# Top rounds ahead of the rotation in attention, first squares ahead of a rounding, retention's last 16 keys as stacked rounded parts

## The reference, cut to what matters

```python
def gated_deltanet_group(q, k, v, ...):
    qkv = jax.nn.silu(causal_depthwise_conv(jnp.concatenate([q, k, v], -1), conv_w))
    ...
    q = l2norm(q.reshape(b, t, DN_HEADS, DN_HEAD_K)) * (DN_HEAD_K ** -0.5)
    k = l2norm(k.reshape(b, t, DN_HEADS, DN_HEAD_K))
...
def dsa_attention(...):                       # 8 heads, one choice of keys for all
    score = jnp.where(admissible[None], score, -jnp.inf)
    _, sel = lax.top_k(score, k_top)          # k_top = 128 of 512 keys for each query
    p = jax.nn.softmax(...)                   # over the 16 meta keys and the chosen ones
...
def retention(q, k, v):                       # 4 heads, 528 keys, values 512 wide
    # y[q] = sum over keys k <= q of decay**(q - k) * (q . k) * v[k]
    y = y * lax.rsqrt(jnp.mean(y * y, axis=-1, keepdims=True) + EPS)
...
y = rmsnorm_2(h, final_norm)
return y[:, N_META:]
```

## Time and profile before

| | |
|---|---|
| median of 3 runs | 2015.24 us (2015.1 to 2015.66) |
| the profiled execution | 2013.44 us, of which the span is 2011.6 us |
| granted TensorE clock, mean over the span | 0.998 |
| PE busy | 1988.7 us, 99% |
| POOL, DVE, ACT busy | 939.3, 861.9 and 738.4 us |

### The profile page before, as it was taken

The page is one execution under the profiler, slowest core; times in us unless marked ns, Lnnn a source line. Parts: engine busy times, 40 slices in busy tenths (PEclk is TensorE's granted clock), DMA queues, the critical chain, the costliest instruction groups (busy, mean ns, idle before and its releaser), DMA issues.

```text
span 2011.6 us, 30211 instructions
## 1 busy us (share of the span) xinstructions
PE 1988.7 (99%) x11374; PEld 1703.1 (85%) x11374; DVE 861.9 (43%) x1495; ACT 738.4 (37%) x1124; POOL 939.3 (47%) x1220
## 2 busy tenths in 40 slices
PE   9999999999999999999999999999999999999998
PEld 6788777899999998788998888888888888888887
DVE  7844776722222225976442243343334552222112
ACT  5633555522222224534444242323333332222222
POOL 6332211554545655453332545354544665454564
PEclk9999999999999999999999999999999999999999
DMA  5211111232222322231111312222222222222222
GB/s 200 74 63 51 37 36 37 74 105 85 92 94 86 103 97 102 74 104 44 65 66 55 125 53 96 78 90 74 89 84 74 94 94 90 98 93 95 95 104 84
DMA packets 49898, 168.68 MB, mean 84 GB/s; under 512 B 6416, under 2 KB 8592, under 8 KB 49808
## 3 DMA queue, kind: packets, MB, share of 16 engines
q1 hardware_dynamic: 46336, 161.37, 23.8%
q10 hardware_dynamic: 3472, 6.03, 0.9%
HBM read 165.29 MB, written 2.10 MB: 83 GB/s over the span
## 4 chain that ended last, share of the span: by engine, by line
PE 92%; DVE 5%; ACT 1%; issue 1%; DMA 0%; DVEq 0%; ACTq 0%
PE slot L2077 91%; DVE qkv L1444 1%; DVE x_lo L1855 0%; DVE xt L1847 0%; PE slot L2523 0%; DVE qkv L1441 0%; PE slot L2257 0%; PE slot L2222 0%; DVE slot L1438 0%; DMA small<-small_in 0%; ACT mixed_hi L947 0%; DVE square L1838 0%; DVE ix_score L1885 0%; DVE xt L1403 0%; DVE top L1881 0%
## 5 line engine op out<-in xcount | busy, mean ns | idle before, releaser
L2599 POOL TENSOR_TENSOR w_lo<-w_raw,w_hi 128x256 fp32r<-128x256 f32 x1216 | 939.1, 805 | 1061.7 <-ACT w_hi L826 803.0
L2077 PE MATMUL slot<-x_hi,w_hi 128*128 128x264 f32 (+1 forms) x1864 | 641.4, 344 | 0.9 <-DVE x_lo L1855 0.7
L2077 PE MATMUL slot<-x_hi,w_lo 128*128 128x264 f32 (+1 forms) x1864 | 629.3, 338 | 0.0
L2077 PE MATMUL slot<-x_lo,w_hi 128*128 128x264 f32 (+1 forms) x1864 | 627.7, 337 | 0.0
L2077 PEld LDWEIGHTS slot<-x_hi,w_hi 128*128 128x128 f32 x1864 | 350.9, 188 | 48.5 <-issue 8.0
L2077 PEld LDWEIGHTS slot<-x_hi,w_lo 128*128 128x128 f32 x1864 | 350.9, 188 | 38.1 <-issue 1.8
L2077 PEld LDWEIGHTS slot<-x_lo,w_hi 128*128 128x128 f32 x1864 | 350.0, 188 | 39.1
L826 ACT ACTIVATE w_hi<-w_raw 128x1024 fp32r<-128x1024 f32 x215 | 225.4, 1054 | 314.6 <-PE slot L2077 306.9
L2077 PE MATMUL slot<-f_hi,w_hi 128*128 128x264 f32 (+2 forms) x550 | 173.5, 316 | 0.0
L2077 PE MATMUL slot<-f_hi,w_lo 128*128 128x264 f32 (+2 forms) x550 | 173.3, 315 | 0.0
L2077 PE MATMUL slot<-f_lo,w_hi 128*128 128x264 f32 (+2 forms) x550 | 172.9, 314 | 0.0
(11 more groups left out here) (351 smaller groups left out, 2863.6 us busy)
## 6 DMA issues: line engine op xcount, KB each, us to landing
w_raw<-weights SPq DMA_DIRECT2D x303, 512.0 KB, 3.2
h<-x_t ACTq DMA_DIRECT2D x4, 512.0 KB, 6.2
dec<-decays ACTq DMA_DIRECT2D x4, 264.0 KB, 3.2
const<-consts SPq DMA_DIRECT2D x1, 576.0 KB, 6.3
at_rot<-rotations ACTq DMA_DIRECT2D x1, 528.0 KB, 5.3
ix_rot<-rotations ACTq DMA_DIRECT2D x1, 528.0 KB, 6.6
rt_rot<-rotations ACTq DMA_DIRECT2D x1, 528.0 KB, 3.8
w_raw<-weights SPq DMA_DIRECT2D x2, 256.0 KB, 4.1
```

The source lines that it names most:

```text
L2077: return nc.tensor.matmul(out, lhsT, rhs, start=start, stop=stop)
L2599: nc.gpsimd.tensor_tensor(w_lo[j][:, piece], w_raw[j][:, piece], w_hi[j][:, piece].bitcast(F32), ALU.subtract).then_inc(s_lo, 1)
```

## The change

1. Attention: of the 8 late rounds of `top([3])` two now stand ahead of step 0, one in each of the steps 0 to 4 ahead of the projections of that step, and one behind those of step 0. `admit(3)` moves from step 4 to step 5.
2. First projections: ACT makes the squares of tiles 0 and 1 ahead of the rounding `x_high(1, 5, M)`.
3. Retention: the matmul for the last 16 keys takes rounded parts. Two new tiles hold them one above the other at partitions 0, 32 and 64: values hi, hi, lo and scores hi, lo, hi, with zeros between. It has 96 rows and is of the short form. DVE gets two memsets once and, for each head, four small instructions; ACT gets two copies of 16x512 for each head; PE gets a wait for them at the first value tile.
4. The end: the halves stay. The table load for `Ln` and `Exp` moves ahead of the last projection, the rounding of the last (padding) weight block behind the last `Exp`, and with it POOL's four pieces. The second half is multiplied as 4, 2, 1 and 1 tiles of 256 columns, where it was 2, 2, 3 and 1, and stored as 4, 2 and 2, the first of the stores by SP.

```diff
-OUT_PARTS = [(0, 2), (2, 4), (4, KD - 1), (KD - 1, KD)]
+LAST_COLS = [(0, 256), (256, T)]
+OUT_PARTS = [[(0, 2), (2, 4), (4, KD - 1), (KD - 1, KD)], [(0, 4), (4, 6), (6, KD - 1), (KD - 1, KD)]]
+OUT_MADE = [sum(len(parts) for parts in OUT_PARTS[:a]) for a in range(len(OUT_PARTS))]
+STORES = [[(0, 2), (2, 4), (4, KD - 1), (KD - 1, KD)], [(0, 4), (4, 6), (6, KD)]]
...
-TOP_LATE = {0: 2, 1: 2, 2: 2, 3: 1, 4: 1}
+TOP_AHEAD = 2
+TOP_WITHIN = {0: 1, 1: 1, 2: 1, 3: 1, 4: 1}
+TOP_BEHIND = {0: 1}
+ADMIT_STEP = 5
...
                 else:
+                    nc.scalar.preload_act_table_set(LN_EXP)
                     for j in range(KD - 1):
...
-                    w_split(BLOCKS_PADDED - 1)
...
                 if j >= 3:
                     x_high(1, j - 3, M)
+            A.sync()
+            squares(srcs[0:2])
             ahead(("qkv", 8))
             x_high(1, 5, M)
-
-            A.sync()
-            squares(srcs[0:2])
...
+                        act.wait_ge(s_rst, 5 * hd + 5)
+                        act.wait_ge(s_last, hd + 1)
+                        A.sig(nc.scalar.activation(rvm_parts[32:32 + M, :], rvm[0:M, :], ACT.Copy), s_rvmhi, 2 * hd + 1)
+                        A.sig(nc.scalar.activation(rvm_parts[0:M, :], rvm[0:M, :], ACT.Copy), s_rvmhi, 2 * hd + 2)
                     made["table"] = None
                     copy_out(("rg", hd, j), rg[j], ACT.Silu)
...
+            w_split(BLOCKS_PADDED - 1)
+            a, (c0, c1) = len(LAST_COLS) - 1, LAST_COLS[-1]
+            for k0, k1 in STORES[a][1:]:
+                act.wait_ge(s_y, out_made(a, k1))
+                act.dma_start(out_dram[:, k0:k1, c0:c1], h[:, k0:k1, M + c0:M + c1]).then_inc(s_out, 16)
...
             admit(2)
+            for _ in range(TOP_AHEAD):
+                top([3])
             for s in range(ATT_STEPS + 3):
...
+                for _ in range(TOP_WITHIN.get(s, 0)):
+                    top([3])
                 for key, _ in filled(s):
                     projected(key)
-                for _ in range(TOP_LATE.get(s, 0)):
+                for _ in range(TOP_BEHIND.get(s, 0)):
                     top([3])
-                if s == max(TOP_LATE):
+                if s == ADMIT_STEP:
                     admit(3)
...
+                V.own(nc.vector.tensor_copy(rstm_parts[0:M, :], rstm[0:M, :]))
+                V.own(nc.vector.tensor_copy(rstm_parts[64:64 + M, :], rstm[0:M, :]))
+                V.sync()
+                V.own(nc.vector.tensor_tensor(rstm_parts[32:32 + M, :], rstm[0:M, :], rstm_parts[0:M, :].bitcast(F32), ALU.subtract))
+                dve.wait_ge(s_rvmhi, 2 * hd + 2)
+                V.sig(nc.vector.tensor_tensor(rvm_parts[64:64 + M, :], rvm[0:M, :], rvm_parts[0:M, :].bitcast(F32), ALU.subtract),
+                      s_last, hd + 2)
...
-                    m = mm(ps[:, T - M:T], rvm[0:M, d * P:d * P + P], rstm[0:M, 0:M], False, True)
+                    if d == 0:
+                        pe.wait_ge(s_last, hd + 2)
+                    m = mm(ps[:, T - M:T], rvm_parts[0:96, d * P:d * P + P], rstm_parts[0:96, 0:M], False, True)
```

More of the change, by code:

```diff
@@ L204, in ffn_results @@
         if (i, d) == (2, KD - 1):
-            add(("down", i, "first half"))
-            add(("norm", 4))
+            for a in range(len(LAST_COLS) - 1):
+                add(("down", i, ("part", a)))
+                add(("norm", 4 + a))
         add(("down", i, d), 3)
@@ L742, in build, with out_made @@
         rs0, squares0 = dsz[:, 0, :], [dqk[:, k, :] for k in range(KD)]
+        def out_made(a, k):
+            return OUT_MADE[a] + sum(k1 <= k for _, k1 in OUT_PARTS[a])
         def halves(ap):
@@ L1320, in _ @@
             ffn(2, M)
-            for a in range(2):
+            act.wait_ge(s_rsd, made["rs"])
+            for a, (c0, c1) in enumerate(LAST_COLS):
                 key = ("norm", 4 + a)
-                if a == 0:
-                    nc.scalar.preload_act_table_set(LN_EXP)
-                    act.wait_ge(s_rsd, made["rs"])
                 wait_result(act, key)
-                half = rs[0][:, a * 256:a * 256 + 256]
-                A.sig(nc.scalar.activation(half, slot(key)[:, 0:256], ACT.Ln, bias=eps[:, 0:1], scale=1.0 / D), *evac_at(key))
+                part = rs[0][:, c0:c1]
+                A.sig(nc.scalar.activation(part, slot(key)[:, 0:c1 - c0], ACT.Ln, bias=eps[:, 0:1], scale=1.0 / D), *evac_at(key))
                 A.sync()
[L1330 to L1333, removed]
-            act.wait_ge(s_out, 16 * 2 * len(OUT_PARTS))
+                A.sig(nc.scalar.activation(part, part, ACT.Exp, scale=-0.5), s_rs, made["rs"] + a + 1)
+            w_split(BLOCKS_PADDED - 1)
[3 more added lines that the diff above has]
+                act.dma_start(out_dram[:, k0:k1, c0:c1], h[:, k0:k1, M + c0:M + c1]).then_inc(s_out, 16)
+            act.wait_ge(s_out, 16 * sum(len(stores) for stores in STORES))
         @block.vector
@@ L2381, in ffn, with part_sum, beside @@
                     down(j, 0, ("down", i, j), parts)
-                middle = M + T // 2
-                def half_sum(a, last):
+                def part_sum(a, last):
+                    c0, c1 = LAST_COLS[a]
                     ps = begin(("norm", 4 + a)) if not last else slot(("norm", 4 + a))
                     pe.wait_ge(s_acc, SQUARES_BEFORE_LAST + 2 * (KD - 1) + (a + 1 if last else 0))
-                    m = mm(ps[:, 0:256], K("ones"), square[0 if last else 1][:, a * 256:a * 256 + 256], not last, last)
+                    m = mm(ps[:, 0:c1 - c0], K("ones"), square[0 if last else 1][:, c0:c1], not last, last)
                     if last:
                         m.then_inc(s_res, 1)
-                def beside():
-                    half_sum(0, False)
-                    half_sum(1, False)
-                    half_sum(0, True)
-                down(KD - 1, 0, ("down", i, "first half"), [(0, M, middle)], False).then_inc(s_res, 1)
-                down(KD - 1, 0, ("down", i, KD - 1), [(0, middle, TT)], True, beside)
-                half_sum(1, True)
+                for a, (c0, c1) in enumerate(LAST_COLS):
+                    final = a == len(LAST_COLS) - 1
+                    def beside():
+                        part_sum(a - 1, False)
+                        part_sum(a - 1, True)
+                        if final:
+                            part_sum(a, False)
+                    m = down(KD - 1, 0, ("down", i, KD - 1 if final else ("part", a)), [(0, M + c0, M + c1)], final, beside if a else None)
+                    if not final:
+                        m.then_inc(s_res, 1)
+                part_sum(a, True)
             def few_rows(out, k, w):
```

39 lines of the change are left out of this document (26 added, 13 removed).

## The result

The changed kernel takes 1999.67 us (median of 6 runs, 1999.49 to 2000.16), the kernel before in the same comparison 2015.63 us (6 runs, 2015.1 to 2017.14). The ratio is 0.9921, with a 95% interval from 0.9911 to 0.9931: 16 us less. The forecast was 2000.5 us. The profiled execution of the changed kernel takes 2000.04 us, its span is 1998.2 us.

The account below looks back on a forecast made before the run. PE, busy 99%, was taken to bound the kernel, so time comes from its matmuls, its few waits or the end. The terms -6.2 - 6.7 - 2.7 + 0.9 = -14.7 gave a median of 2000.5 us, range 1998 to 2005.

Parts of the forecast that it names:

- Part 1: Attention: moving the rounds removes both PE stalls on `att_lo`, 4.1 us idle and about 2 more; -6.2 us, bounds 0 and -6.2.
- The two margins: Attention: estimated room of `att_lo` ahead of PE's need, 3 us at step 4 and about 1 us at step 6.
- Part 2: Retention: the short-form stacked matmul saves 0.42 us in each of sixteen value tiles; -6.7 us, bounds 0 and -6.9.
- The cover: Retention: ACT's copies and DVE's small instructions fit their idle time, parts ready two us before PE wants them; 0 us.
- Part 3: First projections: squares made earlier remove PE's 2.99 us wait, leaving a later one of 0.3; -2.7 us, bounds -1.1 and -3.2.
- I take the difference from the one and give the forecast against the other: Whole kernel: gains summed on the profiled execution, 2013.44 us, then forecast against the median, 2015.24, 1.8 above it.
- Part 4: The end: DVE's last products slow beside POOL's padding pieces, partly offset at the last store; +0.9 us, bounds -0.3 and +1.8.
- The term for the last store: The end: the last store has no other store in front of it in ACT's queue for 0.4 us; -0.3 us.
- (a): Rival, retention: the stacked matmul is no cheaper; 2007.2 us, chance 0.09.
- (c): Rival, first projections: the first squares give nothing, as DVE becomes what PE waits for; 2003.2 us, chance 0.08.
- (d): Rival, retention: the parts come late, PE waiting at each head's tile 0; about 2018 us at 5 us late, chance 0.03.
- (b): Rival, attention: a stall stays, 2003.4 us on average, or 2006.7 if both stay; chance 0.12.

## Why the prediction was right, point by point

**What bounds the kernel** held: PE is 99% busy in both, and every gain lay in its waits, in a cheaper matmul or at the end.

**Part 1** was right in place and size: -6.2 forecast, 30.52 to 24.34 us by the traces, 6.4 by the medians. Of it 4.1 are idle time and 1.7 the low clock. The two rounds ahead of step 0, for which it found 3 us of room, were not needed. The two margins were right too. The `att_lo` that step 4 waits for ends at 913.49 in the changed kernel, 3.0 us ahead of PE's 916.49 (3 forecast); that of step 6 ends at 927.71, 1.0 ahead of 928.75 (1 forecast):

```profile
913.21 0.28 DVE L1980 TENSOR_TENSOR att_lo<-slot,att_hi 128x128 fp32r<-128x128 f32 x1
...
927.43 0.28 DVE L1980 TENSOR_TENSOR att_lo<-slot,att_hi 128x128 fp32r<-128x128 f32 x1
```

**Part 2** had the right mechanism and one price too low. A head's stretch from its first value tile to the end of the fourth went from 9.94 us (1176.26 to 1186.20) to 8.46 (1167.82 to 1176.28), 0.37 for a tile and not 0.42. Counted on to the next head's first value tile it is 1.52 us a head, so the term is -6.1, not -6.7. The failed step is "I put the stacked one 0.11 behind the twelfth and the next tile 0.11 behind it". The starts come as written, even earlier, but the second matmul of the next tile then follows 0.31 us behind the first and not 0.23. A start that comes early behind a narrow matmul is made up for at the next step, so a sum over starts has to run from one tile to the same point of the next, which gives 2.05. This isn't special to the stacked matmul: with it moved away, a tile's first wide matmul stands behind one of 144 columns, and its second follows 0.28 us later (1169.42 to 1169.70). That the price doesn't depend on the place and is 0.115 us for one more was shown by two experiments. By the medians undoing the part costs 6.3. The cover held. ACT made both copies in its idle time, DVE's last part was ready at 1167.50, and PE wanted it at 1169.71, 2.2 us later (2 forecast):

```profile
1165.48 0.63 ACT L1307 ACTIVATE last_value_parts<-const 16x512 fp32r<-16x512 f32 x1 [0.46 <-DVEq L2045]
...
1168.02 0.60 ACT L897 ACTIVATE rg_early<-slot 128x512 f32<-128x512 f32 x1 [1.25 <-PE slot L2118]
```

```profile
1166.82 0.68 DVE L2055 TENSOR_TENSOR last_value_parts<-const,last_value_parts 16x512 fp32r<-16x512 f32 x1
```

The rule of the Trainium skill that the rows of a weight load don't set its time ("TensorE: Matmul & The Clock Gate", "Part 2: What happens when you issue a matmul") agrees: one of 96 rows cost 0.115 us here, one of 128 rows 0.11.

**Part 3** was right in the trace to a tenth: the wait at 66 us is gone, one of 0.28 us stands at 74.67 (0.3 forecast), and the stage ends 2.7 us earlier. Its worth in the medians, 4.7, was missed. The step that failed stands in the forecast's first part: "I take the difference from the one and give the forecast against the other". The profiled execution of before was one of those in which the clock stays up behind the squares' stall, and the timed ones mostly weren't. The 1.8 us by which their median was longer were not a constant of the measurement. The traces give 1.6 of them to the low clock behind this stall, and that went with it.

**Part 4** had the right sign and nearly the right size: +0.9 forecast, 1.1 to 1.2 measured. The step that was off is "about two of three meet one: +1.2": three of DVE's instructions met pieces of POOL (the first ended at 1992.78, soon after POOL's start at 1992.55), and each lost about 0.5 us, not 0.6: two took 1.21 and 0.94 where 0.68 and 0.42 is their time alone (the kernel with the padding block put back), and the last one 0.94 for 0.48. That is 1.5. The term for the last store held: it is issued 1.5 us later and lands 2.17 us after its issue where it was 2.54, so -0.4 (-0.3 forecast). What the forecast didn't see is that this depends on the delay: with the products fast again, the same stores stand close together, and 0.4 of the gain is lost. The Trainium skill's rule of turns on the shared port ("SBUF — State Buffer", "Who interferes with whom") has the direction right, and the order of the ends looks like turns: POOL's pieces end at 1993.37, 1994.49 and 1995.36, DVE's three instructions at 1993.91, 1994.78 and 1995.64 (spans on POOL are rough). By it I had +2.1, a whole piece for each; the whole delay of DVE was 1.5.

**The sum.** By the traces -6.2 - 6.1 - 2.7 + 1.1 = -13.9, less 0.4 for the chance wait at 806 us: 13.5, and the spans differ by 13.4. By the medians of the kernels with one part undone 6.4 + 6.3 + 4.7 - 1.2 = 16.2, and the medians differ by 16.0. That agreement is closer than the measurement: the interval of the ratio is 4 us wide, and the median of the kernel before went from 2014.97 to 2016.51 from one set of runs to the next. The forecast's 14.7 came near by luck in part, since two errors cancel: 0.8 us too much gain in parts 2 and 4, and 2 too little for the clock. Against the profiled execution, where the low clock at 70 us plays no part, the sum promised 1.3 us too much (1998.7 forecast, 2000.04 measured), of which 0.4 is the chance wait. Of the rivals, (a), (c) and (d) did not come. The price of (d) at 5 us late is summed wrong: by its own terms 5 less 2 of room and 1.7 for the clock are 4.7 a head, about 2019.3 and not 2018. (b) came in none of the changed kernel's profiles, and was seen, as two waits of 0.8, only with the rounds placed otherwise.

## What to carry to other kernels

A stall of TensorE has a price beside its idle time: the matmuls at half clock behind it. Whether they come differs from one execution to the next, so a single profile can miss 1.6 us of a stall's worth; a median above the profiled execution is a reason to look for such a stall. Put the work that fits into a wait ahead of the instruction that waits: with eight rounds of 1.5 us there no stall was left, and with two ahead of the loop and six behind that instruction two stalls of 0.8 us were. At the very end of a kernel look at what runs beside the last products: here padding did, and the old end, with the padding block first and a small last store, was 1.2 us faster.

## What the runs showed of the hardware that was not expected

The fall of the clock to 0.50 followed a stall in some executions and not in others. Behind 2.24 to 2.26 us at 916 to 923 us it fell in all four profiles that have this stall; behind 2.99 us at 66 us in two of four; behind 1.8 us at 932 to 939 us in none of four; behind 0.83 and 0.85 us not. So the idle time alone doesn't decide. The low clock lasted about 3.4 us each time. In attention and behind the squares' stall it cost 1.6 to 1.7 us of PE's time, by the starts of the same instructions in two traces.

The kernel's start can have it too. In the profile with the rounds ahead of step 0 alone, a wait of 2.19 us for the first weights was followed by 0.50; a wait of 2.04 there, in the changed kernel's second profile, was not:

```profile
9.00:10.00 1.00, 0.07 (x1) 0.10 (x1) 0.73 (x2) 1.00 (x3) 1.00 (x2) 1.00 1.03 387
...
11.00:12.00 1.00, 1.00 (x4) 0.80 (x3) 1.00 (x2) 1.00 (x3) 1.00 (x1) 0.50 0.66 241
```

There it cost nearly nothing. PE starts on these weights at 9.93, 1.30 us later than in the profile with all rounds ahead of the rotation (8.63). Behind the low clock it is 2.2 us late, and by 20 us 1.3 again. So this execution was 1.0 us above its kernel's median because the first weights came late, and not because of the clock.

DVE beside POOL lost about 0.5 us on each of three instructions, less than one of POOL's pieces, which took 0.7 alone (2.83 for four) and 0.92 beside DVE (3.67 for four).
